# Up products of the feed-forward part on tokens that are not yet normalised, the factor put on in PSUM, and the weights' rounding split in halves

## The reference, cut to what matters

```python
    x = x + merged @ w_o                       # w_o: 1024 x 1024
    h2 = rmsnorm(x, ln2)                       # x * r(token) * ln2(feature)
    u = causal_dwconv(h2 @ w_up, conv_w, conv_b)   # w_up: 1024 x 5632; 3 taps along the tokens
    a, b = jnp.split(u, 2, axis=-1)
    return x + (jax.nn.silu(a) * b) @ w_down   # w_down: 2816 x 1024
```

## Time and profile before

| | |
|---|---|
| median of 3 runs | 904.84 us (903.73 to 905.35) |
| the profiled execution | 904.53 us, of which the span of the profile is 902.5 us |
| PE busy | 832.2 us (92%) |
| DVE busy | 495.0 us (55%) |
| ACT busy | 377.9 us (42%) |
| granted TensorE clock, mean | 0.98 |
| feed-forward part, from up(0) | from 709.33 us to 896.56 us of the span |

### The profile page before, as it was taken

How to read it: one execution, slowest core, us unless ns; L and a number is a source line. 1 busy time by engine, 2 the same in 40 slices (tenths; PEclk the granted TensorE clock), 3 DMA queues, 4 the chain that set the end, 5 groups by cost and what they waited for, 6 DMA issues and landing times.

```text
span 902.5 us, 13987 instructions
## 1 busy us (share of the span) xinstructions
PE 832.2 (92%) x5603; PEld 673.0 (75%) x5603; DVE 495.0 (55%) x770; ACT 377.9 (42%) x523; POOL 89.9 (10%) x113
## 2 busy tenths in 40 slices
PE   4989999999999997965698899999999899999997
PEld 4989789989998633312332699877777799999995
DVE  5899577854564511100110576555775577667585
ACT  5333454465334211001011565456554366556462
POOL 4222000122000000000000101122170000000000
PEclk9999999999999999988899999999999999999999
DMA  8665556225778999999999995434636446546511
GB/s 280 231 199 188 187 181 238 96 94 188 261 289 347 420 421 421 421 422 422 423 421 405 330 211 190 166 117 185 161 120 229 168 141 233 186 142 227 189 47 47
DMA packets 95436, 217.51 MB, mean 241 GB/s; under 512 B 14047, under 2 KB 44893, under 8 KB 83609
## 3 DMA queue, kind: packets, MB, share of 16 engines
q1 hardware_dynamic: 94697, 215.59, 66.3%
q10 hardware_dynamic: 576, 0.92, 0.3%
q0 software_dynamic: 112, 0.30, 0.3%
HBM read 215.44 MB, written 1.34 MB: 240 GB/s over the span
## 4 chain that ended last, share of the span: by engine, by line
PE 70%; DMA 12%; DVE 10%; ACT 3%; issue 2%; SPq 1%; POOL 1%; DVEq 0%; POOLq 0%; ACTq 0%
PE ps L912 16%; PE ps L914 16%; PE ps L913 16%; DMA moe_ring<-in_w_expert_in 10%; PE ps L1394 7%; PE ps L1298 6%; DVE w_lo L1782 3%; PE ps L1263 1%; PE ps L1324 1%; PE ps L1318 1%; DMA stage<-in_w_in 1%; PE ps L1104 1%; PE ps L1114 1%; DMA h_tok<-in_x 1%; ACT w_odd L1476 1%
## 5 line engine op out<-in xcount | busy, mean ns | idle before, releaser
L914 PE MATMUL ps<-x_hi,w_lo 128*128 128x256 f32 x568 | 162.2, 286 | 0.0
L1782 DVE TENSOR_TENSOR w_lo<-stage,w_hi 128x2048 fp32r<-128x2048 f32 (+1 forms) x44 | 101.9, 2354 | 25.3 <-ACT w_hi L1476 23.7
L914 PEld LDWEIGHTS ps<-x_hi,w_lo 128*128 128x128 f32 x568 | 110.6, 195 | 0.0
L912 PE MATMUL ps<-x_hi,w_hi 128*128 128x256 f32 x360 | 104.9, 291 | 3.9 <-DVE w_lo L1782 3.0
L913 PE MATMUL ps<-x_lo,w_hi 128*128 128x256 f32 x360 | 103.5, 287 | 0.0
L1476 ACT ACTIVATE w_hi<-stage 128x2048 fp32r<-128x2048 f32 (+1 forms) x44 | 79.2, 1849 | 55.1 <-PE ps L914 49.2
L912 PEld LDWEIGHTS ps<-x_hi,w_hi 128*128 128x128 f32 x360 | 70.8, 197 | 4.7 <-issue 2.8
L913 PEld LDWEIGHTS ps<-x_lo,w_hi 128*128 128x128 f32 x360 | 71.0, 197 | 0.1
L913 PE MATMUL ps<-w_lo,x_hi 128*128 128x512 f32 (+1 forms) x168 | 63.8, 379 | 0.0
L912 PE MATMUL ps<-x_hi,w_odd 128*128 128x256 f32 x216 | 61.5, 285 | 1.3 <-DVE x_lo L1768 1.3
L913 PE MATMUL ps<-x_lo,w_odd 128*128 128x256 f32 x216 | 61.1, 283 | 0.0
(11 more groups left out here) (398 smaller groups left out, 2041.2 us busy)
## 6 DMA issues: line engine op xcount, KB each, us to landing
stage<-in_w_in SPq DMA_DIRECT2D x23, 2048.0 KB, 8.1
moe_ring<-in_w_expert_in SPq DMA_DIRECT2D x38, 1024.0 KB, 18.3
moe_ring<-in_w_expert_out SPq DMA_DIRECT2D x16, 1024.0 KB, 17.6
stage_b<-in_w_up SPq DMA_DIRECT2D x12, 1024.0 KB, 7.5
stage<-in_w_down SPq DMA_DIRECT2D x11, 1024.0 KB, 5.1
stage<-in_w_up SPq DMA_DIRECT2D x10, 1024.0 KB, 9.0
up_odd<-in_w_expert_in SPq DMA_DIRECT2D x8, 1024.0 KB, 18.3
down_odd_a<-in_w_expert_out SPq DMA_DIRECT2D x6, 1024.0 KB, 24.5
```

What stands on the lines that cost most here:

```text
L912: mm(out, still[0], moving[0], start=first, stop=False)
L914: return mm(out, still[1], moving[0], start=False, stop=last)
L1782: tt(lo[:, cols], staged(n)[:, cols], hi[:, cols].bitcast(fp32), ALU.subtract).then_inc(lo_ready, 1)
```

## The change

The transposes of `norm(3)` are taken from the tokens as they are. New "at" steps ft 0 to 3 transpose `h_tok` (16 transposes), ScalarE and VectorE read them out as `f_hi`, `f_lo` with the gain ln2. ft 0 and 1 (features 0 to 511) stand between wo2 2 and wo2 3; ft 2 and 3 are filled within up(0). `up(0)` becomes `first_up`: all four output tiles over the first half of the input features, then all over the second half. The factor r(token) is made as before, but goes by two small matmuls ("frow") and a copy into `r_row`, the same 256 numbers on every partition; VectorE multiplies the up products of every unit by it in PSUM, two instructions of 128x512 a unit, ahead of the taps. The residual is copied into PSUM after up(0). In the units of the hardware loop, the splitting of the up weights of unit u+2 is divided: its first half stands at the start of the unit, ahead of the taps on ScalarE and ahead of the conv on VectorE; its second half stays at the end. A dummy Silu stands ahead of the loop on ScalarE.

```diff
+    steps += [{"op": "ffsplit", "half": 0}, fills[0]]
+    at("ft", 0)
+    at("ft", 1)
+    steps += [{"op": "normtile", "i": 3}, fills[1], {"op": "ffsplit", "half": 1}]
+    for i in range(2, 4):
+        at("ft", i)
+        steps[-1]["inside"] = ("up", 0)
+    steps += [{"op": "norm", "i": 3}, {"op": "ffsplit", "half": 2}]
+    at("frow")
+    steps[-1]["inside"] = ("up", 1)
     steps.append({"op": "ffn"})
...
# TensorE
+                elif kind == "ft":
+                    eng.wait_ge(h_ready, (6, 8)[i // 2])
+                    for t in range(NT):
+                        for m in range(2):
+                            k = 2 * i + m
+                            last = eng.transpose(ps[:, bank, m * S + t * P:m * S + (t + 1) * P], h_tok[:, t, k * P:(k + 1) * P], ident[:, :])
+                elif kind == "frow":
+                    eng.wait_ge(frow_ready, 1)
...
+                def first_up():
+
+                    w = parts(ff_pair(1))
+                    eng.wait_ge(ff_lo, 1)
+                    wait_read(eng, "at", "ft", 1)
+                    for half in range(2):
+                        if half == 1:
+                            inner_at(1)
+                            eng.wait_ge(ff_lo, 2)
+                            wait_read(eng, "at", "ft", 3)
+                        for n, m in enumerate((2, 3, 0, 1)):
...
+                            if (half, n) == (0, 0):
+                                inner_at(0)
+                    last.then_inc(ff_up, 1)
...
-                up(0, 0)
+                first_up()
+                for t in range(NT):
+                    residual_into_psum(t)
...
# ScalarE, the unit
                 def unit(u, p):
                     if isinstance(u, int) and u == FFN_UNITS - 3:
                         ff_split_up(u + 2, p)
-                    eng.wait_ge(ff_up, u + 1)
+                    elif not isinstance(u, int):
+                        ff_split_up(u + 2, p, (0,))
                     for m in range(4):
+                        if m % 2 == 0:
+                            eng.wait_ge(ff_scaled, u * 2 + m // 2 + 1)
...
                     if not isinstance(u, int):
-                        ff_split_up(u + 2, p)
+                        ff_split_up(u + 2, p, (1,))
...
-                ff_split_up(1, 1)
+                act(silu_cell, half_neg[:, 0:1], ACT.Silu)
...
# VectorE, the unit
                 def unit(u, p):
+                    eng.wait_ge(ff_up, u + 1)
+                    for b in range(2):
+                        wide = ps[:, 2 * p + b, :].rearrange("p (m t) -> p m t", m=2)
+                        tt(wide, wide, r_row[:, :].unsqueeze(1).broadcast_to([P, 2, S]), ALU.mult).then_inc(ff_scaled, 1)
                     if isinstance(u, int) and u == FFN_UNITS - 3:
                         ff_split_up(u + 2, p)
+                    elif not isinstance(u, int):
+                        ff_split_up(u + 2, p, (0,))
                     eng.wait_ge(ff_tap, u + 1)
...
                     if not isinstance(u, int):
-                        ff_split_up(u + 2, p)
+                        ff_split_up(u + 2, p, (1,))
```

More of the change, by code:

```diff
@@ L231, in schedule @@
         at("mt", i)
-        steps[-1]["inside"] = True
+        steps[-1]["inside"] = ("wo2", 0)
     steps.extend(unit("wo2", 0, [0, 1]))
     fills = unit("wo2", 1, [2, 3])
-    steps += [{"op": "ffsplit", "half": 0}, fills[0], {"op": "normtile", "i": 3}, fills[1], {"op": "ffsplit", "half": 1},
-              {"op": "norm", "i": 3}]
+    steps += [{"op": "ffsplit", "half": 0}, fills[0]]
[8 more added lines that the diff above has]
+    steps[-1]["inside"] = ("up", 1)
     steps.append({"op": "ffn"})
@@ L341, in two_blocks @@
         ya_lo = at_kib("ya_lo", 128, [P, KT, S], r32)
+        wide_g2 = qk[:, 3 * D:4 * D]
         v_tok = at_kib("v_tok", 136, [P, NT, D])
@@ L344, in two_blocks @@
         su_tok = su[:, :, :].rearrange("p f t -> p (f t)").rearrange("p (t d) -> p t d", t=NT)
-        wide_g2 = su[:, 0:4, :].rearrange("p f t -> p (f t)")
+        f_hi = at_kib("f_hi", 136, [P, KT, S], r32)
+        f_lo = at_kib("f_lo", 144, [P, KT, S], r32)
         ys_lo = at_kib("ys_lo", 144, [P, KT, S], r32)
@@ L420, in two_blocks @@
         m8, top2, ss_half, gain2, half_ms = cell(16), cell(16), cell(4), cell(KT), cell(NT)
-        sgu_mv, sgu_st = cell(4), cell(24)
+        sgu_mv, sgu_st, silu_cell = cell(4), cell(24), cell(1)
         logf, lf2, cum = cell(8), cell(8), cell(8)
@@ L986, in fill_pj @@
                     for inner in steps:
-                        if inner.get("inside"):
+                        if inner.get("inside") == (kind, 0):
                             fill_at(inner)
@@ L1123, in fill_at @@
                                   start=True, stop=True)
+                elif kind == "ft":
[7 more added lines that the diff above has]
+                    for t in range(NT):
+                        last = mm(ps[:, bank, t * P:(t + 1) * P], rstd[:, t:t + 1].broadcast_to([P, P]), ident[:, :],
+                                  start=True, stop=True)
                 elif kind == "xn":
@@ L1370, in ffn, with inner_at @@
                     eng.sem_inc(primed, 1)
+                def inner_at(which):
+                    for s in steps:
+                        if s.get("inside") == ("up", which):
+                            fill_at(s)
+                def first_up():
[8 more added lines that the diff above has]
+                        for n, m in enumerate((2, 3, 0, 1)):
+                            bank, c0 = m // 2, m % 2 * S
+                            if half == 0 and m % 2 == 0:
+                                fills = sum(1 for s in steps if s["op"] == "pj" and s["n"] % 4 == bank)
+                                eng.wait_ge(pj_free[bank], fills)
+                            for k in range(half * KT // 2, (half + 1) * KT // 2):
+                                for b, f in ((0, 0), (0, 1), (1, 0)):
+                                    last = mm(ps[:, bank, c0:c0 + S], w[b][:, k, m * P:(m + 1) * P], (f_hi, f_lo)[f][:, k, :],
+                                              start=(m % 2, k, b, f) == (0, 0, 0, 0), stop=(k, b) == (KT - 1, 1),
+                                              skip_group_check=True)
+                            if (half, n) == (0, 0):
+                                inner_at(0)
+                    last.then_inc(ff_up, 1)
                 def up(u, p):
@@ L1378, in up @@
                     for m in range(4):
-                        last = by_features(2 * p + m // 2, (m % 2) * S, w, m * P)
+                        last = by_features(2 * p + m // 2, (m % 2) * S, w, m * P, x=(f_hi, f_lo))
                     last.then_inc(ff_up, 1)
@@ L1399, in down @@
                         last.then_inc(ff_down, 1)
-                up(0, 0)
+                first_up()
+                for t in range(NT):
+                    residual_into_psum(t)
+                wait_read(eng, "pj", "wo2", 3)
                 with eng.Fori(0, (FFN_UNITS - 3) // 2) as i:
@@ L1417, in _ @@
                     fill_at(cur)
-                elif cur["op"] == "norm":
+                elif cur["op"] == "norm" and cur["i"] != 3:
                     norm(cur["i"])
@@ L1452, in norm @@
             def norm(i):
-                if i != 2:
-                    for t in range(0 if i == 0 else 1, NT):
+                if i == 0:
+                    for t in range(NT):
                         squares_of(i, t)
@@ L1546, in evac_at @@
                         act(x_hi[:, k, :], src[:, m * S:(m + 1) * S], ACT.Copy, scale=vec[:, C_LN1 + k:C_LN1 + k + 1]).then_inc(xn_hi, 1)
-                elif kind == "rrow":
+                elif kind == "ft":
+                    eng.wait_ge(at_full, n + 1)
+                    for m in range(2):
+                        k = 2 * i + m
+                        act(f_hi[:, k, :], src[:, m * S:(m + 1) * S], ACT.Copy, scale=vec[:, C_LN2 + k:C_LN2 + k + 1]).then_inc(ft_hi, 1)
+                elif kind in ("rrow", "frow"):
                     eng.wait_ge(at_full, n + 1)
@@ L1641, in log_sigmoid, with ff_split_up @@
                 act(lf2, lf2, ACT.Ln).then_inc(ln_f, 1)
-            def ff_split_up(u, p):
+            def ff_split_up(u, p, halves=range(2)):
                 eng.wait_ge(ff_up_in[p], (u - p) * 16 + 32)
@@ L1649, in ff_split_up @@
                     eng.wait_ge(pj_full, units[len(units) - 2 + u]["read"])
-                for half in range(2):
+                for half in halves:
                     cols = slice(half * KT * UNIT // 2, (half + 1) * KT * UNIT // 2)
@@ L1705, in _ @@
                         ff_split_up(0, 0)
-                elif s["op"] == "norm":
+                    elif s["half"] == 1:
+                        squares_of(3, 1)
+                    else:
+                        ff_split_up(1, 1)
+                elif s["op"] == "norm" and s["i"] != 3:
                     norm(s["i"])
@@ L1752, in norm_tile @@
```

(16 more changed lines are left out.)

6 lines of the change are left out of this document (2 added, 4 removed).

## The result

The changed kernel takes 935.9 us (median of 4 runs, 934.9 to 937.1) against 905.1 us; the ratio is 1.0344, with a 95% interval of 1.0332 to 1.0356. The profiled execution took 935.3 us, its span is 933.5.

The account below looks back on a forecast made before the run. TensorE was taken to bound the kernel before, a ring of loads and splits after. On 904.53: -2.4 + 0.9 + 23.4 + 6.4 = +28.3; the walk of starts, +27.9, was taken: 932.5 us, range 921 to 939.

Parts of the forecast that it names:

- What bounds the kernel: Feed-forward loop: TensorE full, 16.98 us a unit; the load of up weights is the thing to watch.
- The front end: From wo2 3 to up(1): 8.1 us leaves TensorE's path, transposes, residual copies and small matmuls enter; gain 2.4 us.
- the ring: Loop: up-weight load, half-splits, conv and split_down, which lets SP ask for the next load; 20.9 us against TensorE's 16.98.
- the load of unit 0's half-split: Start of the loop: unit 0 has its weights, asked for early, so no wait was put there.
- The factor in PSUM: Each unit's two VectorE multiplications by the token's factor: 0.70 us each, 1.4 a unit, costing nothing in the loop.
- the landing: From split_down's end to up weights usable in the loop: 11.0 us.
- The first turn: Units 0 and 1: up(3)'s weights usable 21.0 us after first_up's end; down(1) waits 0.9 us.
- Down(1) to down(7), and the tail: Down(2) to down(7) wait 3.9 us each, 23.4; after the units written out, down(10) waits 6.4.
- Weights in time: Rival for the loop: weights arrive in time, TensorE stays full, only the front end counts, 902.1 us; chance 0.07.
- A quicker load: Rival for the up-weight loads: 423 GB/s instead of 358, ring 19.5 us, total 922 us; chance 0.07.
- A lower clock: Rival: the clock falls to 0.83 in TensorE's new gaps, +2.8 us, total 935 us; chance 0.05.
- Table loads that stay: Loads ahead of the taps survive the dummy Silu: 0.9 us in four units, up to 3.5 more, 936 us; no chance given.

Follow-up runs that it names:

- the run with SyncE's order: Changed kernel, but SyncE asks for the up weights of unit u+1 ahead of the wait for split_down that guards unit u's down weights: 902.06 us, ratio 0.9966.
- the kernel with fewer bytes: Changed kernel loading only the first 128 of the 256 rows of each unit's down weights (512 instead of 1024 KB): 927.8 us, ratio 1.0242.

## Why the prediction was right

Measured 935.9 (935.3 in the profiled execution), predicted 932.5, range 921 to 939. The mechanism was the one forecast; the sum was 2.8 us short of the profiled run. By its own steps:

- *What bounds the kernel.* Right, and so was the choice of what to watch. Before, ScalarE stood idle 6.29 us for a DMA in unit 8 and it cost nothing, being hidden behind two up products; the change made the same wait the rule.
- *The front end, -2.4.* first_up ended at 715.64 against 714.9, but wo2's additions already came 0.74 us later in this execution (691.31 against 690.57), before anything of the change runs. So first_up's end was right to a tenth. The residual copies were put at 3.45 and took 3.04 (715.64 to 718.68), so without that drift up(1) starts at 717.94 and not at 718.4: the front end is worth 2.9, not 2.4. In this kernel the difference is lost in the ring; in the run with SyncE's order it shows (902.06 against 904.92). Left out was the load of unit 0's half-split: "asked for early", it came with 0.3 us too little, which cost 0.1.
- *The factor in PSUM, 0.70 each.* 0.692 each (median of 22), 1.29 for the pair, as the second starts before the first has ended; and nothing in the loop, shown by leaving it out (ring closed) and by doubling it (ring open).
- *The ring, 20.9 us.* 21.07. ScalarE's and VectorE's terms were right (4.16 from the half-split's start at 737.90 to the conv at 742.06, against 4.25). Short was the landing: 11.0 was put, 11.14 to 11.39 were measured in seven turns. Over the six turns from down(1) to down(7) the landings make 1.6 us more and the engines' terms 0.6 less, together 1.0.
- *The first turn.* Landing took 12.15 us there (725.75 to 737.90), 1.15 more than put. SyncE's instruction for these loads is 2.48 us long in the trace (the others 1.00); what held it is not shown. The same turn took 12.18 in the run without the factor and 11.22 in the run without the dummy Silu.
- *Down(1) to down(7), and the tail.* From down(7)'s start to down(10)'s it was 45.57, put at 45.8. But TensorE's idle time there is not the 6.4 ahead of down(10): up(10) also waits, 1.86 us, for the conv of unit 8 to leave its PSUM banks, which I had not listed, and down(10) 2.33. The other 2 us are products that ran longer, nearly all of it in the window 896 to 908 at a granted clock of 0.86. The start of down(10) is set by VectorE, so how TensorE's wait is divided did not matter.

The differences are 0.74 drift, 0.1 in unit 0, 1.15 first landing, 1.0 in the six turns and 0.3 at the last down (5.74 us at a granted clock of 1.00, put at 5.47), less 0.2 in the tail and 0.3 behind the last product: 2.8. The 0.74 is no step of the prediction: wo2's first addition starts anywhere from 689.97 to 691.31 in the traces of this case, whatever the kernel.

The rivals. *Weights in time, 902.1*: this is what the kernel does once the ring is opened at SyncE (902.06), so its condition was the right one, and its cost nearly: the gain is 2.9 and not 2.4, and that the two times agree to 0.1 is partly chance, as the kernel before ran at 904.92 beside it and not at 904.53. *A quicker load*: refuted, every full landing took over 11.1 us. The Trainium skill's fit ("DMA: Bandwidth & Descriptors", section "Anatomy of one DMA"), which the page gives for loads issued by GpSimd, would give 9.2 us from the issue of the down weights; the turn shown took 11.2 (747.87 to 759.09). With the same page's limit of about 358 GB/s for loads from memory (section "Where 436 GB/s comes from") and the fixed 2.0 of the fit, an estimate from the Trainium skill is 8.8 us for 3.15 MB and 10.8 together, nearer to what was measured. *A lower clock*: it happened, and cost nothing that can be seen: the start of down(10) is set by VectorE, and down(10) ran at 1.00. In the six turns TensorE was busy 110.72 us for products that take 6 x 16.98 = 101.9 at full clock, at a mean granted 0.93; the 8.8 us more came out of its waits (idle 15.7 instead of 24.5), because the ring set the pace. *Table loads that stay*: put at 0.9 for each even unit with the load ahead of the taps; measured 1.4 (turns of 22.44 against 21.07), since the load moves ahead of the half-split with the code. The Trainium skill's 2.66 us for a switch ("ScalarE: Activation LUTs", section "What ACT_TABLE_LOAD costs") is not seen: the half-split starts 1.30 behind the load's start. Nor does a drain show ahead of a load: in unit 2 of the kernel before, ScalarE's split of the down weights ends at 757.29, the load starts at 757.31 and Silu at 758.60.

## What to carry to other kernels

When a step is moved to an earlier place, ask what its first wait is and how the thing waited for is set off: here the wait for a load was put ahead of the very instruction that lets the load's queue go on, and a cover of 11 us became a ring of 21. Idle time that a profile shows for free, like the 6.29 us in unit 8 before, prices such a move before it is made. The ring was opened here in two ways, by the place of the split and by the order of two loads in SyncE's queue; the second is on an engine that the change doesn't touch.

## What the runs showed of the hardware that was not expected

- The granted clock fell in places where TensorE was idle no longer than 2 to 4 us at a time (0.67 over 770 to 780, around the end, at 771.03, of a wait of 3.99 us), and waits of 2.10 and 2.27 us, ahead of 834.00 and 855.11, were followed by stretches at 0.65 (834 to 836) and 0.66 (855 to 860). The front end of the kernel before, with two waits of 1.26 and 1.28 us and small products, kept 1.00. The windows of the kernel with fewer bytes have two microseconds at 0.50, the lower of the clock's two levels (1.2 GHz), over 770 to 772, right behind its wait of 4.35 us ahead of 768.65.
- VectorE multiplies in place in PSUM, source and target the same bank, at 0.692 us for 128x512 (22 instructions of the changed kernel, 0.689 to 0.699), the same as from PSUM to SBUF (0.692).
- With half a megabyte less ahead of them, the same up weights were there 9.6 to 10.1 us behind `split_down` in five turns, where it had been 11.1 to 11.4, and 11.0 to 11.8 us in the other three. Not explained.
